# Two layers of a hybrid decoder trunk on one core: output tile 7 of the prompt moves from the border of the last sample into step 8 of the sample before

## The reference

```python
s_s = einsum('btgrd,btgkjd->btgrkj', q, ks) * sc     # 16 selected blocks of 64 tokens
p_s = masked_softmax(s_s, mask_s)
o_s = einsum('btgrm,btgmd->btgrd', p_s, vs)
p_w = masked_softmax(einsum('btgrd,bsgd->btgrs', q, kw) * sc, mask_w)   # the last 512 tokens
o_w = einsum('btgrs,bsgd->btgrd', p_w, vw)
o = g[..., 0] * o_c + g[..., 1] * o_s + g[..., 2] * o_w
return x + gate * einsum('bte,ed->btd', o * silu(z), w_out)
```

## Time and profile before

| | |
|---|---|
| median of 3 runs | 1251.34 us (1250.05 to 1251.96) |
| the profiled execution: span from first to last instruction | 1244.8 us, 25178 instructions |
| the profiled execution: its own time as a run | not given beside the profile; the median lies 6.5 us above its span |
| mean granted TensorE clock | 0.978 |
| busy, share of the span | PE 94%, DVE 39%, ACT 34%, POOL 16% |
| samples' sparse attention with its tiles | 1003.5 to 1223 us of the span |
| end of the kernel after it | 1223 to 1244.8 us |

### The profile page before, as it was taken

One profiled execution on the slowest core, in us unless ns is written; L12 is line 12 of the kernel. 1 busy time (PEld: TensorE's weight loads), 2 busy tenths in 40 slices (PEclk: granted clock), 3 DMA queues, 4 the chain that ended last, 5 costly groups with the idle time before them and its releaser, 6 DMA issues. The chain is left out here.

```text
span 1244.8 us, 25178 instructions
## 1 busy us (share of the span) xinstructions
PE 1173.2 (94%) x9085; PEld 735.4 (59%) x9085; DVE 487.0 (39%) x1496; ACT 424.7 (34%) x1076; POOL 204.5 (16%) x345
## 2 busy tenths in 40 slices
PE   4899999999999899999999899999999789999995
PEld 1677764676767657567787455555555344444552
DVE  1534032344532340202300755665665524343345
ACT  3322112233320131010111465666656334444452
POOL 0000000000000001102100322222222434444300
PEclk9899999999989989999989999999999989999997
DMA  9654434303053122225001966666674999999972
GB/s 380 272 203 193 163 133 166 136 1 136 1 223 124 71 78 70 75 71 192 8 1 39 360 228 233 238 230 215 236 272 156 303 351 355 356 354 355 356 264 77
DMA packets 96551, 238.76 MB, mean 192 GB/s; under 512 B 12714, under 2 KB 50732, under 8 KB 91948
## 3 DMA queue, kind: packets, MB, share of 16 engines
q1 hardware_dynamic: 73036, 164.95, 37.6%
q0 software_dynamic: 23392, 72.21, 16.3%
HBM read 227.57 MB, written 17.05 MB: 197 GB/s over the span
## 5 line engine op out<-in xcount | busy, mean ns | idle before, releaser
L410 PE MATMUL ps<-arena,wring 128*128 128x288 f32 x1664 | 425.0, 412 | 3.6 <-ACT arena L546 2.0
L410 PEld LDWEIGHTS ps<-arena,wring 128*128 128x128 f32 x1664 | 314.3, 192 | 101.6 <-issue 14.0
L1649 POOL DMA_DIRECT2D arena<-in_cmp_pages x128 | 70.3, 550 | 269.4 <-PE ps L1814 100.8
L419 PE MATMUL ps<-wring,arena 128*128 128x512 f32 x192 | 92.8, 618 | 6.3 <-DMA arena<-in_narrow_c 6.3
L1742 DVE CUSTOM_DVE_ANT_0 wring<-ps,wring 128x128 f32<-128x128 f32 (+3 forms) x128 | 57.6, 487 | 72.0 <-PE ps L1671 70.2
L2219 DVE CUSTOM_DVE_ANT_1 arena<-ps,small 128x512 f32<-128x512 f32 x64 | 44.3, 693 | 88.3 <-PE ps L2136 88.2
L1734 ACT ACTIVATE wring<-ps 128x128 f32<-128x128 f32 (+3 forms) x128 | 49.1, 436 | 86.5 <-PE ps L1694 86.5
L1720 ACT ACTIVATE wring<-wring 128x128 f32<-128x128 f32 (+3 forms) x128 | 70.7, 559 | 8.6 <-DVE wring L1742 8.6
L2195 ACT ACTIVATE arena<-arena 128x512 f32<-128x512 f32 (+1 forms) x88 | 56.9, 648 | 47.5 <-DVE arena L2235 47.5
L2206 ACT ACTIVATE arena<-ps 128x512 f32<-128x512 f32 x72 | 43.0, 598 | 80.0 <-PE ps L2157 80.0
L1807 PE MATMUL ps<-arena 128*32 128x256 f32 x1024 | 69.5, 389 | 0.7 <-issue 0.7
(11 more groups left out here) (397 smaller groups left out, 1536.8 us busy)
## 6 DMA issues: line engine op xcount, KB each, us to landing
wring<-in_weights SPq DMA_DIRECT2D x27, 2048.0 KB, 9.1
arena<-in_cmp_pages SPq DMA_DIRECT2D x128, 256.0 KB, 3.5
arena<-in_cmp_pages POOLq DMA_DIRECT2D x128, 256.0 KB, 4.5
wring<-in_kv_pages SPq DMA_DIRECT2D x64, 256.0 KB, 11.0
wring<-in_kv_pages POOLq DMA_DIRECT2D x64, 256.0 KB, 7.1
arena<-in_kv_pages SPq DMA_DIRECT2D x50, 256.0 KB, 8.2
arena<-in_kv_pages POOLq DMA_DIRECT2D x50, 256.0 KB, 7.0
out_win_k_out<-in_win_kv SPq DMA_DIRECT2D x8, 512.0 KB, 12.1
```

The lines of the kernel that those rows point to most:

```text
L410: last = pe.matmul(out[:, 0:HT], w[:, k, ct * P:ct * P + P], moving[k][:, half * HT:half * HT + HT], start=(k == 0), stop=(k == KT - 1))
L419: last = pe.matmul(main, tokens, w[:, k, :], start=(k == 0), stop=(k == KT - 1))
L1649: eng.dma_start(cring[q % CR][:, 2 * half + j, :], v["cmp_pages"][bass.ds(ids[2 * d + j], 1)] .rearrange("o p c -> (o p) c")).then_inc(c_i ...
```

## The change

`LAST_TILE_PAIR, LAST_TILE_AT = 3, 8` are new. Tile 7 (KT - 1) is taken from the start of sample 7 and put into sample 6 (NB - 2). On PE it stands at step 8, ahead of that step's turn. On DVE its addition and its square stand after the scores of i = 6 of sample 7, which are done in sample 6. On SP its weights are requested in sample 7's loads, after the fourth pair and ahead of the window. Tiles 0 to 6 stay where they were.

```diff
+        LAST_TILE_PAIR, LAST_TILE_AT = 3, 8
...
                 for n in range(NB):
                     for pair in range(NG // 2):
                         load_kv(sp, 0, n, pair)
+                        if n == NB - 1 and pair == LAST_TILE_PAIR:
+                            sp.wait_ge(tile_done, KT - 1)
+                            sp.dma_start(lohi_[:, 0:1024], v["out_tiles"][KT - 1]).then_inc(tile_in, 16)
...
                     load_window(sp, 0, n)
-                    if n:
+                    if 0 < n < NB - 1:
                         sp.wait_ge(tile_done, n)
                         sp.dma_start(lohi_[:, 0:1024], v["out_tiles"][n]).then_inc(tile_in, 16)
...
                 for n in range(NB):
-                    pe_out_tile(pe, n)
+                    if n < NB - 1:
+                        pe_out_tile(pe, n)
                     if n:
                         pe_out_turn(pe, n - 1)
                     for at in range(NJ + 1):
+                        if n == NB - 2 and at == LAST_TILE_AT:
+                            pe_out_tile(pe, KT - 1)
                         if at <= LAST:
                             pe_turn(pe, n, at)
...
                     if n:
                         dve_combine(dve, n - 1)
-                    dve_out_tile(dve, n)
+                    if n < NB - 1:
+                        dve_out_tile(dve, n)
                     if n:
                         dve_out_gate(dve, n - 1)
                     for i in range(NJ):
                         if n < NB - 1:
                             dve_scores(dve, n + 1, i)
-                        if i == 3:
+                        if i == 3 and n < NB - 1:
                             dve_square(dve, n)
+                        if i == LAST_TILE_AT - 2 and n == NB - 2:
+                            dve_out_tile(dve, KT - 1)
+                            dve_square(dve, KT - 1)
```

## The result

The changed kernel takes 1257.2 us in the median of 15 runs (1252.32 to 1261.98), the kernel before 1250.57 us in 15 runs (1246.8 to 1255.17). The ratio is 1.0041, with a 95% interval of 1.0025 to 1.0057, or 5.1 us of 1250.57 (3.1 to 7.1): slower, as forecast, and 6.3 us lies inside. The ratio is taken over all runs of both; the two medians alone lie 6.6 us apart. The interval also holds the 4.3 us of the rival without the clock, so the time alone doesn't tell the two apart; the trace has to.

What follows compares the result with a forecast made beforehand. PE's order was taken to bound the kernel; 3.9 bubble + 0.1 DVE + 0.2 weights + 0.1 cold turn + 2.0 clock = 6.3 us slower, from 1251.34 to 1257.6 us, range 1253.6 to 1261.5.

Steps and rivals of the forecast that it cites:

- the rival without the clock: Border of samples 6 and 7: the bubble stands but the clock stays at 1.00; 4.3 us slower, 1255.6 us, chance 0.14.
- The tile's move is worth nothing in itself: PE, step 8 of sample 6: the tile costs the same 6.97 us there, with no bubble to fill.
- The uncovered chain, 3.9 us: Border of samples 6 and 7: without the tile, PE waits for DVE's combining from 1200.43 to 1204.3, 3.9 us.
- 0.1 for DVE's additions: DVE, sample 7's scores of steps 6 and 7: three added operations delay the window's scores by about 0.1 us.
- 3.5 to 4.2 that I had named as a sign: PE at the border: 3.5 to 4.2 us idle before the turn, released by DVE's combining, would show the forecast.
- The weights, 0.2 us: PE at step 8: weights requested 0.62 us earlier land at 1194.3 to 1195.0; wait of 0 to 0.3, taken as 0.2.
- The rival of late weights: Step 8: weights take 11.3 us to land, PE waits 3.2 us; 9.5 us slower, 1260.8 us, chance 0.10.
- SP's queue and the output rows at nothing: SP: the added wait delays nothing; output rows requested 7 us later still land over 10 us early; cost nothing.
- The clock, 2.0 us: Sample 7's first steps: low granted clock behind the bubble costs 2.0 us, bounds 0 and 3.4.
- 0.1 for a cold turn: PE's turn at the border starts cold, 0.47 us instead of 0.27; taken as 0.1 us.
- The row against the term: Kernel's start: a 2.59 us bubble before 22.13 left the clock at 1.00, which spoke against the 2.0 us clock term.
- 6.5 us outside the span: Whole run: median 1251.34 us against a profiled span of 1244.8, so some 6.5 us lie outside and were left unchanged.

Runs made afterwards that it cites:

- The filler: Changed kernel plus four products (3.5 us) that no output depends on, at the border ahead of the turn; ratio 1.0048 to the kernel before.
- the shorter chain: Changed kernel with DVE's combining cut in two, its operations on the exponentials' sums moved behind the scores of i = 5; ratio 1.0011 to the kernel before.
- Three more traces with one bubble at this border: Changed kernel with DVE's part undone (ratio 1.0027), with the tile at step 7 (1.005), with the combining cut in two (1.0011), each to the kernel before.
- the half tiles: Kernel before with tile 7 split: four products at step 8 of sample 6, four at the border, DVE's part as before; ratio 1.002.

## Why the prediction was right, point by point

- *The tile's move is worth nothing in itself*: right, 6.97 us at both places, and no wait ahead of it.
- *The uncovered chain, 3.9 us, and 0.1 for DVE's additions*: 3.81 in all. The filler (31.72 for 31.69 with 3.5 us more work) and the shorter chain (1.0 us off the bubble) show that the chain on DVE is what the tile had hidden. The 0.1 for DVE was not there: its window scores start 3.55 us behind those of i = 6 (1204.93 to 1208.48), as the 3.54 before. PE's new tokens' scores did start 0.24 late (27.79 us behind the turn of sample 5, where 20.58 and the tile's 6.97 make 27.55), inside DVE's time as foreseen; this is why the idle time reads 3.45 and falls just short of the 3.5 to 4.2 that I had named as a sign.
- *The weights, 0.2 us*: none. They landed 1.0 us early. The rival of late weights stands one step or one sample away: 2.31 us at step 7, 1.37 us in sample 5.
- *SP's queue and the output rows at nothing*: right, by the experiment that moves the request alone, and PE read the output rows without a wait.
- *The clock, 2.0 us, and 0.1 for a cold turn*: the mechanism came, and this is the term that was mis-sized: 0.92 us behind the bubble, the cold turn in them. I had built the 2.0 on the low stretch of 6.8 us beside the last border; here the clock was low only from about 1212.0 to 1215.4. Three more traces with one bubble at this border lost about as much (0.94, 1.11 and 1.08), the run with two moved tiles 2.25 and 2.27. So the term is real, and 0.9 to 2.3 is what these traces show of it; that it goes away when PE is kept busy was shown with the filler. The tail, which I had left as it was, took 0.62 longer in this trace, by chance as far as can be told.
- *The row against the term, a bubble of 2.59 us that left the clock at 1.00*: misread. The column reads 1.00 there, but the matmuls are slow on both sides of that bubble: 16 of L392 take 3.64 us before it (15.90, below) and behind it (22.13, rows 6), and groups of the same shapes are faster from about 30 us on. PE's timeline of the kernel before:

```profile
15.90 3.64 PE L392 MATMUL ps<-wring,arena 128*32 128x512 f32 x16 [15.90 <-DMA wring<-in_weights]
...
25.71 1.88 PE L370 MATMUL ps<-fixed,arena 128*128 128x9 f32 x8
...
31.97 1.06 PE L370 MATMUL ps<-fixed,arena 128*128 128x9 f32 x8
32.96 1.93 PE L392 MATMUL ps<-arena 128*32 128x512 f32 x16
```

  1.88 against 1.06 and 3.64 against 1.93 are about half speed. So PE was slow before the bubble came, the column's 1.00 at the start of the span doesn't tell PE's speed, and the rival of a bubble without the clock had no row behind it.
- *The rule of the Trainium skill* ("TensorE: Matmul & The Clock Gate", section "What's actually happening") that such a penalty is under 1% of a typical span, varies from run to run and shouldn't be fitted: the traces agree with it, for 0.92 to 2.27 us are 0.07 to 0.18% of the span, and they vary. For a change of this size it still can't be left out: it was 0.92 of the 4.73 us at the border.
- *6.5 us outside the span*: wrong, without consequence for the difference. The profiled run of the changed kernel took 1253.02 with a span of 1251.3, so 1.7 lie outside; the rest of the 6.5 is that the median of the kernel before lies above its profiled execution.

By the trace the border costs 3.81 + 0.92 = 4.73 us, 5.35 with the tail of this one run, where 6.3 were forecast; the ratio gives 5.1.

## What to carry to other kernels

Work that stands between two dependent stages may be paying for a chain on another engine: before moving it, follow what runs below it, and price the move by what that chain lacks afterwards, not by the length of the work. Half of the work was cover enough here; and where nothing can be moved in, cutting the chain itself (operations that don't need the last result go ahead of it) takes time off as well (1.0 and 1.5 us per bubble here). A bubble on PE can be dearer than its length when matmuls follow: 0.9 to 2.3 us more here.

## What was not expected of the hardware

The clock also falls where PE has no idle time. In the run with the half tiles, four stretches far ahead of the change (from 227, 261, 295 and 329 us) have a mean clock of 0.83 over 10 us with PE busy for all of it, where the kernel before has 1.00 in the same places; the longest wait of PE between 220 and 345 us is 0.6 us. The matmuls agree with the column: 38 records instead of 48 in the first of them. Two of the four, as stretches of that kernel:

```profile
227.00:237.00 10.00, 10.00 (x38) 6.55 (x39) 2.41 (x7) 2.62 (x7) 0.00 (x0) 0.83 0.78 333
261.00:271.00 10.00, 10.00 (x38) 6.69 (x38) 3.35 (x9) 2.83 (x4) 0.00 (x0) 0.83 0.00 0
```

0.17 x 10 us x 2 = 3.4 us at the 1.2 GHz level, of which half, 1.7 us, is lost: 6.8 us for four of them. That run reached the turn of sample 5 at 1189.78, 10.3 us after the kernel before, and most of it is this. It may be why runs of one kernel lie 10 us and more apart: the mean granted clock of the runs goes with their time (for the half tiles 0.977 in the quickest, 1245.43 us, and 0.969 in the slowest, 1257.51, which is the run of this trace). It is also why distances inside one trace tell more than two medians when the question is of 5 us. What sets off these stretches was not found.
